# The last layer behind its mixers on 576 instead of 592 columns: the meta columns are left out

## The chip, the cores and the metric

The kernel runs on one core of a Trainium2 chip. The metric is the device time of one launch in microseconds. TensorE (PE) multiplies, VectorE (DVE) and ScalarE (ACT) do the elementwise work, GpSimd (POOL) and SyncE (SP) issue the transfers.

## The reference, cut to what matters

Two layers of a decoder trunk run over a prompt of 512 tokens with 16 learned meta tokens ahead of it, and over 8 sample sequences of 8 tokens that share the weights: 64 + 16 + 512 = 592 tokens, which are the columns of every activation in the kernel. Each layer is

```python
h = h + 0.5 * swiglu(rmsnorm(h, w['norm_ffn1']), ...)
x = rmsnorm(h, w['norm_mix']);  z = x @ w['w_in'] + w['b_in']
# four mixers: conv, retention, gated linear attention (GLA), differential attention
gate = jax.nn.sigmoid(gates.reshape(B, L, N_BRANCH, D_MODEL))
merged = jnp.einsum('blnc,ncd,blnd->bld', branches, w['w_branch'], gate)
h = h + merged @ w['w_out']
h = h + 0.5 * swiglu(rmsnorm(h, w['norm_ffn2']), ...)
...
y_prompt = h_p[:, N_META:]
```

The meta tokens are dropped from the result `y`. In the mixers they are keys, values and states that the later tokens read, and their keys and values are outputs of both layers; behind the mixers of the last layer nothing reads them.

## The kernel before

Activations lie transposed: 128 partitions hold a tile of 128 channels, and the 592 tokens are the columns, ordered sample (64, `TS`), meta (16, `META`), prompt (512). A product runs in two halves of `HALF` = 296 columns, one PSUM bank each. Every float32 product is made of three reduced products (high times high, low times high, high times low), so each value exists as a high and a low part: `x_hi`/`x_lo` (the layer's input), `w_hi`/`w_lo` (a weight unit of 8 blocks of 128x128), `hid_hi`/`hid_lo`, `br_hi`/`br_lo`, `m_hi`/`m_lo`. ScalarE makes the high part, VectorE the low one.

SP streams the weights, 512 KB a unit, into a ring of four slots (`w_raw`); `split_high` (ACT, L773) and `split_low` (DVE, L1984) prepare a unit, TensorE multiplies it in `products` (L1362): 8 blocks x 3 products x 2 halves = 48 matmuls. The feed-forwards use another scheme (`ffn`, L1391): for each of 22 pairs of gate and up tiles seven products of 4 blocks x 3 matmuls, on operands that are sums and differences of the two halves of the columns (`x_half`, tiles of `HALF` columns in `x_hi`, `x_lo` and `x_more`), with VectorE forming the sums of weights and the quarters of the result. The steady pairs run in a hardware loop.

The order of a layer, written out by hand for each engine and tied by semaphores: first feed-forward and its down projection (3 units for each of 8 output tiles), `project` (values, then 18 tiles of `z`), attention of the samples, attention of the prompt, retention, GLA, head norms, merge, output projection, second feed-forward, its down projection. Of the 32 tiles of branch gates 24 are "early": TensorE makes them block by block between the steps of the mixers (`early_gates`, L1362 through `products`), ScalarE takes their tanh into `hT[:, 0:4]` (`gate_activated`, L1117), and SP stores them to DRAM (`gate_rows`) and fetches them back for the merge; the first five tiles of the residual `hT` are spilled to `h_rows` meanwhile. In `gates` each of 8 output tiles takes a late gate tile (48 matmuls) and the products of the four branches (4 x 12), merged by VectorE (L2793, L2798, L2803). `head_norms` sums squares over heads by products with a matrix of ones (`sum_tile`, L1374, full float32, two records each), ScalarE makes the inverse roots.

At the end `last_tiles` (DVE) adds the last output tile in two halves (L2318, L2320), and SP stores `y_out` tile by tile behind the last weight load (L639), the last tile in two halves (L641, L643).

`product` in `ffn`, `products` and `sum_tile` set TensorE's widths; in the other engines each operation names its own slice (`room`, `HALF`, `T`).

## Time and profile before

| | us |
|---|---|
| median of three runs | 2823.16 |
| lowest, highest | 2822.53, 2825.8 |
| the profiled execution | 2824.82 |
| its span, first to last instruction | 2823.2 |

The profile is of one execution, so its times are summed against its own 2824.82 us. In a timeline a row's second number is the duration of the merged group, which for pipelined matmuls overlaps the next one: the time of one matmul is better taken from the length of a run divided by its count. "<-" behind an idle time names what ended it.

### The profile page before, as it was taken

The page shows a single profiled execution, that of the slowest core. Times are in us where ns is not written, and L with a number is a line of the kernel's source. Part 1 is how long each engine was busy: PE and PEld are TensorE (multiplying, and loading weights), DVE is VectorE, ACT ScalarE, POOL GpSimd, SP SyncE. Part 2 cuts the span into 40 slices and gives each one's busy share as a digit, 9 for nine tenths or more (in the row PEclk, how much of TensorE's full clock was granted, in tenths as well). Part 3 has the DMA queues.
Part 4 walks back from the last instruction along what each step waited for, and adds up shares of the span by engine and source line. Part 5 has one row for each costly group of instructions (what it writes and reads, how often), then busy time and mean ns, then how long its engine had stood idle before and what let it go on. Part 6 is the DMA issues. An engine that isn't in the chain of part 4 may idle for free.

```text
span 2823.2 us, 57804 instructions
## 1 busy us (share of the span) xinstructions
PE 2798.5 (99%) x21860; PEld 2711.6 (96%) x21860; DVE 1992.6 (71%) x3588; ACT 1208.0 (43%) x2156; POOL 120.6 (4%) x218
## 2 busy tenths in 40 slices
PE   8999999999999999999999999999999999999999
PEld 7999999988899999999999999999888899999999
DVE  8889534477667688886488894346776676988942
ACT  6445323435334254454254462234353433554521
POOL 0000001230000000000000000012300000000000
PEclk9999999999999999999999999999999999999999
DMA  4222325562234312223222232255623343122232
GB/s 137 98 95 97 105 67 190 159 225 90 98 112 168 123 54 95 98 89 112 82 72 92 89 105 97 93 166 172 214 87 113 126 153 108 68 89 89 104 99 101
DMA packets 103024, 320.00 MB, mean 113 GB/s; under 512 B 13615, under 2 KB 30415, under 8 KB 101312
## 3 DMA queue, kind: packets, MB, share of 16 engines
q1 hardware_dynamic: 90576, 277.03, 28.5%
q0 software_dynamic: 12272, 40.56, 4.5%
q8 instruction: 119, 1.95, 0.3%
q14 instruction: 57, 0.47, 0.1%
HBM read 289.76 MB, written 29.12 MB: 113 GB/s over the span
## 4 chain that ended last, share of the span: by engine, by line
PE 96%; DVE 2%; SPq 1%; issue 1%; ACT 1%; DMA 0%; DVEq 0%; ACTq 0%
PE ps L1362 50%; PE ps L1391 35%; PE ps L1568 3%; PE ps L1374 2%; PE ps L1637 1%; PE ps L1849 1%; PE ps L1670 0%; PE ps L1715 0%; PE ps L1735 0%; DVE Z L2496 0%; PE ps L1689 0%; DMA w_raw<-wstream 0%; PE ps L1619 0%; PE ps L1796 0%; SPq L563 0%
## 5 line engine op out<-in xcount | busy, mean ns | idle before, releaser
L1984 DVE TENSOR_TENSOR w_lo<-w_raw,w_hi 128x1024 fp32r<-128x1024 f32 x240 | 292.6, 1224 | 355.1 <-ACT w_hi L773 351.6
L1391 PE MATMUL ps<-x_more,w_hi 128*128 128x296 f32 x2112 | 459.3, 299 | 1.5 <-DVE x_more L2846 1.1
L1391 PE MATMUL ps<-x_hi,w_hi 128*128 128x296 f32 x1408 | 420.6, 299 | 1.3 <-DVE w_lo L2022 1.2
L1391 PE MATMUL ps<-x_hi,w_lo 128*128 128x296 f32 x1408 | 421.6, 299 | 0.0
L1391 PE MATMUL ps<-x_lo,w_hi 128*128 128x296 f32 x1408 | 421.4, 299 | 0.0
L773 ACT ACTIVATE w_hi<-w_raw 128x1024 fp32r<-128x1024 f32 x224 | 234.6, 1053 | 411.4 <-PE ps L1362 243.3
L1362 PE MATMUL ps<-x_hi,w_hi 128*128 128x296 f32 x1600 | 364.9, 309 | 2.8 <-ACT hT L1117 2.8
L2022 DVE TENSOR_TENSOR w_lo<-w_raw,w_hi 128x512 fp32r<-128x512 f32 x440 | 296.9, 689 | 91.2 <-ACT w_hi L821 91.2
L1391 PEld LDWEIGHTS ps<-x_more,w_hi 128*128 128x128 f32 x2112 | 351.0, 188 | 2.7 <-issue 1.6
L1362 PE MATMUL ps<-x_lo,w_hi 128*128 128x296 f32 x1600 | 348.8, 299 | 0.0
L1362 PE MATMUL ps<-x_hi,w_lo 128*128 128x296 f32 x1600 | 348.2, 299 | 0.0
L1391 PE MATMUL ps<-x_more,w_lo 128*128 128x296 f32 x1056 | 314.9, 298 | 0.0
L1362 PE MATMUL ps<-hid_hi,w_hi 128*128 128x296 f32 x1408 | 310.8, 300 | 0.0
L1362 PE MATMUL ps<-hid_hi,w_lo 128*128 128x296 f32 x1408 | 308.9, 298 | 0.0
L1362 PE MATMUL ps<-hid_lo,w_hi 128*128 128x296 f32 x1408 | 308.5, 298 | 0.0
L871 ACT ACTIVATE p_copy<-ps 128x296 f32<-128x296 f32 x264 | 110.1, 418 | 394.8 <-PE ps L1391 394.3
L1362 PEld LDWEIGHTS ps<-x_hi,w_hi 128*128 128x128 f32 x1600 | 258.6, 189 | 18.8 <-issue 14.0
L821 ACT ACTIVATE w_hi<-w_raw 128x512 fp32r<-128x512 f32 x440 | 265.5, 623 | 14.4 <-PE ps L1362 13.8
L1391 PEld LDWEIGHTS ps<-x_hi,w_hi 128*128 128x128 f32 x1408 | 265.7, 189 | 2.3 <-DVE w_lo L2022 1.7
L1391 PEld LDWEIGHTS ps<-x_hi,w_lo 128*128 128x128 f32 x1408 | 265.9, 189 | 0.0
L1391 PEld LDWEIGHTS ps<-x_lo,w_hi 128*128 128x128 f32 x1408 | 264.9, 188 | 0.0
L1362 PEld LDWEIGHTS ps<-x_hi,w_lo 128*128 128x128 f32 x1600 | 260.5, 189 | 0.0
(371 smaller groups left out, 4948.0 us busy)
## 6 DMA issues: line engine op xcount, KB each, us to landing
w_raw<-wstream SPq DMA_DIRECT2D x420, 512.0 KB, 3.7
kpage<-cache_k SPq DMA_DIRECT2D x128, 128.0 KB, 2.8
vpage<-cache_v POOLq DMA_DIRECT2D x128, 128.0 KB, 3.6
gate_rows<-hT SPq DMA_DIRECT2D x48, 296.0 KB, 2.9
d_sg<-gate_rows SPq DMA_DIRECT2D x16, 888.0 KB, 5.0
h_rows<-hT SPq DMA_DIRECT2D x2, 1480.0 KB, 6.3
hT<-h_rows SPq DMA_DIRECT2D x2, 1480.0 KB, 6.6
hT<-h_in SPq DMA_DIRECT2D x4, 592.0 KB, 8.5
```

Source lines behind the costliest of these rows:

```text
L773: act.activation(w_hi[:, slot, :, :], w_raw[:, slot, :, :], ACT.Copy).then_inc(weights_high, 1)
L821: act.activation(w_half(t)[0], w_source(t, g, total), ACT.Copy).then_inc(operands_high, 1)
L871: act.activation(room, ps[:, bank, 0:HALF], ACT.Copy).then_inc(pair_taken, 1)
L1362: mm = pe.matmul(ps[:, 2 * p + half, 0:HALF], wp[:, k, :], xp[:, k0 + k - blocks[0], half * HALF:(half + 1) * HALF], start=start and k == ...
L1374: mm = pe.matmul(ps[:, 2 * p + half, 0:HALF], mat, tile[:, half * HALF:(half + 1) * HALF], start=start, stop=stop)
L1391: mm = pe.matmul(ps[:, bank, 0:HALF], wp[:, k, :], xp, start=new and k == 0 and n == 0, stop=k == KH - 1 and n == 2, skip_group_check=True)
L1568: mm = pe.matmul(ps[0:n, (WINDOWS * g + w) % 8, 0:256], xp[:, k, c0:c0 + n], wp[:, s0:s0 + 2, k, :], start=k == 0 and m == 0, stop=k == KD ...
L1637: mm = pe.matmul(ps[0:n, score_bank(j, g, i), 0:min(ns, 512)], q, k[:, 0:min(ns, 512)], start=True, stop=True)
L1849: mm = pe.matmul(ps[0:cols, h, a0:a0 + count], g_kl[32 * h:32 * h + 32, n % 2, c0:c0 + cols], g_ql[32 * h:32 * h + 32, n % 2, at:at + coun ...
L1984: v.tensor_tensor(w_lo[:, slot, :, :], w_raw[:, slot, :, :], w_hi[:, slot, :, :].bitcast(F32), ALU.subtract).then_inc(weights_low, 1)
L2022: v.tensor_tensor(lo, w_source(t, g, total), hi.bitcast(F32), ALU.subtract).then_inc(weight_steps, 1)
```

## The change

With `MOVED` = 576, every engine keeps a variable `width` that is 296 and becomes 288 (`live_half(l)`) in the last layer when the engine enters the head norms; the early gates take 288 from the start. All slices behind that point use `span()` for `HALF` and `live(ap)` for a whole row of `2 * span()` columns. Since the 16 meta columns lie at 64 to 79, the last 16 prompt columns (576 to 591) are copied into their place at three points: the operands `x_hi`, `x_lo` (ScalarE, behind the last projection tile), the branch tiles in `Z` and `od` (ScalarE, before the head norms), the residual `hT` (VectorE, at the end of the merge). TensorE waits for the first two. The output keeps its layout: SP stores each tile of `y` as 576 columns and the moved 16 columns apart.

```diff
+MOVED = T - META
+def live_half(l):
+    return HALF if l + 1 < DEPTH else MOVED // 2
...
+        width = [HALF]
+        def live_columns(l):
+            width[0] = live_half(l)
+        def span():
+            return width[0]
+        def live(ap):
+            return ap[:, 0:2 * span()]
...
         def pair(p):
-            return ps[:, 2 * p:2 * p + 2, 0:HALF]
+            return ps[:, 2 * p:2 * p + 2, 0:span()]
...  sync
+            live_columns(DEPTH - 1)
             for m in range(KD - 1):
                 sp.wait_ge(residual_added, 4 + 24 * DEPTH - KD + m + 1)
-                sp.dma_start(y_out[:, m:m + 1, :], hT[:, m:m + 1, :]).then_inc(y_stored, 16)
+                sp.dma_start(y_out[:, m, 0:MOVED], hT[:, m, 0:MOVED]).then_inc(y_stored, 16)
+                sp.dma_start(y_out[:, m, MOVED:T], hT[:, m, TS:TS + META]).then_inc(y_stored, 16)
             sp.wait_ge(first_half_added, 1)
-            sp.dma_start(y_out[:, KD - 1, 0:HALF], hT[:, KD - 1, 0:HALF]).then_inc(y_stored, 16)
+            sp.dma_start(y_out[:, KD - 1, 0:span()], hT[:, KD - 1, 0:span()]).then_inc(y_stored, 16)
+            sp.dma_start(y_out[:, KD - 1, MOVED:T], hT[:, KD - 1, TS:TS + META]).then_inc(y_stored, 16)
             sp.wait_ge(residual_added, 4 + 24 * DEPTH)
-            sp.dma_start(y_out[:, KD - 1, HALF:T], hT[:, KD - 1, HALF:T]).then_inc(y_stored, 16)
-            sp.wait_ge(y_stored, 16 * (KD + 1))
+            sp.dma_start(y_out[:, KD - 1, span():MOVED], hT[:, KD - 1, span():MOVED]).then_inc(y_stored, 16)
+            sp.wait_ge(y_stored, 16 * (2 * KD + 1))
...  scalar, tile(l, c)
+                    if l == DEPTH - 1 and c == NZ - 1:
+                        act.activation(x_hi[:, :, TS:TS + META], x_hi[:, :, MOVED:T].bitcast(F32), ACT.Copy)
+                        act.activation(x_lo[:, :, TS:TS + META], x_lo[:, :, MOVED:T].bitcast(F32), ACT.Copy).then_inc(z_ready, 1)
...  scalar, head_norms(l)
                 act.wait_ge(lvl_scores, len(level_items))
+                if l == DEPTH - 1:
+                    act.wait_ge(conv_done, 1)
+                    act.wait_ge(prompt_evac, 10)
+                    act.wait_ge(ret_evac, WINDOWS)
+                    act.wait_ge(gla_evac, WINDOWS)
+                    act.activation(Z[:, RQ:CA, TS:TS + META], Z[:, RQ:CA, MOVED:T], ACT.Copy)
+                    act.activation(od[:, :, TS:TS + META], od[:, :, MOVED:T], ACT.Copy).then_inc(gla_evac, 1)
+                    act.wait_ge(gla_evac, WINDOWS + 1)
+                live_columns(l)
...  tensor
-                            mm = pe.matmul(ps[:, 2 * p + half, 0:HALF], wp[:, k, :],
-                                           xp[:, k0 + k - blocks[0], half * HALF:(half + 1) * HALF],
+                            mm = pe.matmul(ps[:, 2 * p + half, 0:cols], wp[:, k, :],
+                                           xp[:, k0 + k - blocks[0], half * cols:(half + 1) * cols],
...
-                            mm = pe.matmul(ps[:, bank, 0:HALF], wp[:, k, :], xp, start=new and k == 0 and n == 0,
+                            mm = pe.matmul(ps[:, bank, 0:span()], wp[:, k, :], xp, start=new and k == 0 and n == 0,
...
-                    last = products(gate_pair(f), slot, (part, part + 1), part, x_hi, x_lo, start=part == 0, stop=part == 7)
+                    last = products(gate_pair(f), slot, (part, part + 1), part, x_hi, x_lo, start=part == 0, stop=part == 7, n_cols=live_half(l))
...
                         pe.wait_ge(z_ready, NZ + 1)
+                        if l == DEPTH - 1:
+                            pe.wait_ge(z_ready, NZ + 2)
...
                 pe.wait_ge(conv_done, 1)
+                if l == DEPTH - 1:
+                    pe.wait_ge(gla_evac, WINDOWS + 1)
+                live_columns(l)
...  vector
             def head_norms(l):
+                live_columns(l)
...
                 v.wait_ge(h_back, 16)
+                if l == DEPTH - 1:
+                    v.tensor_copy(hT[:, :, TS:TS + META], hT[:, :, MOVED:T])
                 v.drain().then_inc(mixers_left, 1)
```

The rest of the diff replaces `HALF` by `span()`, `HALF:T` by `span():2 * span()` and whole rows by `live(...)` in the steps behind the mixers.

## Rows read from the trace of the kernel before

**Rows 1.** The page: busy us (share) xinstructions, then the clock by slice.
```profile
PE 2798.5 (99%) x21860; PEld 2711.6 (96%) x21860; DVE 1992.6 (71%) x3588; ACT 1208.0 (43%) x2156; POOL 120.6 (4%) x218
PEclk9999999999999999999999999999999999999999
```

**Rows 2.** Busy us by stretch: PE, PEld, DVE, ACT, POOL; then clock, DMA.
```profile
2424.00:2676.00 252.00, 252.00 (x1850) 251.74 (x1849) 227.15 (x405) 132.82 (x257) 0.00 (x0) 1.00 0.26 92
sum 740.00, PE 739.74 PEld 717.66 DVE 519.30 ACT 300.91 POOL 4.98; mean PE 105.68 PEld 102.52 DVE 74.19 ACT 42.99 POOL 0.71
```

**Rows 3.** The chain that ended last, its end: start us, us, what.
```profile
2259.55 164.05 PE ps L1362 x1200
2423.60 8.17 PE ps L1391 x60
2431.77 1.00 PE ps L1374 x4
2432.76 243.48 PE ps L1391 x1788
2676.24 143.75 PE ps L1362 x1056
```

**Rows 4.** The chain in the projection of layer 1: the values, 256 columns.
```profile
1828.45 37.08 PE ps L1568 x315
```

**Rows 5.** Waits of TensorE from 1992 to 2260 us: total, times, longest.
```profile
PE ps L1362 <- ACT hT L1117: 1.4, 3, 0.6
...
PE ps L1796 <- DVE rst L2587: 0.2, 1, 0.2
```

**Rows 6.** Timeline of ScalarE in the head norms, and the chain's ones-sums there.
```profile
2234.97 2.45 ACT L1221 ACTIVATE Z<-Z 128x592 f32<-128x592 f32 x4
2246.06 0.66 ACT L1229 ACTIVATE hn_root<-ps 128x592 f32<-128x592 f32 x1 [1.93 <-PE ps L1374]
...
2241.04 7.97 PE ps L1374 x32
```

**Rows 7.** Timelines of ScalarE and TensorE around the last projection tile.
```profile
2014.10 0.75 ACT L1041 ACTIVATE Z<-ps,prm 128x592 f32<-128x592 f32 x1 [4.97 <-PE ps L1362]
2016.52 0.28 ACT L1096 ACTIVATE s_turn<-ps 128x128 f32<-128x128 f32 x1 [0.15 <-PE ps L1691]
...
2016.38 0.54 PE L1362 MATMUL ps<-x_hi,w_hi 128*128 128x296 f32 x2
2017.31 0.27 PE L1701 MATMUL ps<-ident,s_turn 128*128 128x128 f32 x1
```

**Rows 8.** Timeline of VectorE where the output projection begins.
```profile
2377.71 0.78 DVE L2257 SCALAR_TENSOR_TENSOR hT<-ps,hT 128x592 f32<-128x592 f32 x1 [1.54 <-PE ps L1362]
```

**Rows 9.** Timelines of VectorE and TensorE in the first pair of feed-forward two.
```profile
2438.38 0.69 DVE L2022 TENSOR_TENSOR w_lo<-w_raw,w_hi 128x512 fp32r<-128x512 f32 x1
...
2439.19 0.32 PE L1391 MATMUL ps<-x_hi,w_hi 128*128 128x296 f32 x1
```

**Rows 10.** VectorE's tile groups behind 2260 us, and its idle time in a pair.
```profile
L2137 DVE TENSOR_TENSOR tmp<-ps,p_copy 128x296 f32<-128x296 f32 x44 | 20.2, 459 | 0.0
L2142 DVE TENSOR_TENSOR tmp<-tmp,gu 128x592 f32<-128x592 f32 x22 | 16.9, 769 | 0.0
...
2567.82 0.69 DVE L2022 TENSOR_TENSOR w_lo<-w_raw,w_hi 128x512 fp32r<-128x512 f32 x1 [0.94 <-ACT w_hi L821]
```

**Rows 11.** SP's issues at the end, its wait, and the slowest small load's landing.
```profile
2800.20 5.47 SPq L639 DMA_DIRECT2D y_out<-hT  x7
2812.09 0.33 SPq L641 DMA_DIRECT2D y_out<-hT  x1
SPq L643 <- DVE hT L2320: 8.6, 1, 8.6
aw<-params POOLq DMA_DIRECT2D x2, 8.0 KB, 8.9
```

**Rows 12.** Timeline of VectorE: a slice of 528 of 592 columns.
```profile
1985.71 0.76 DVE L2496 SCALAR_TENSOR_TENSOR Z<-Z,prm 128x528 f32<-128x528 f32 x1
```

More of the change, by code:

```diff
@@ L870, in copy @@
                 def copy(room, bank):
-                    act.activation(room, ps[:, bank, 0:HALF], ACT.Copy).then_inc(pair_taken, 1)
+                    act.activation(room[:, 0:span()], ps[:, bank, 0:span()], ACT.Copy).then_inc(pair_taken, 1)
                 def pair_(N, quad, j, kind, tile):
@@ L1116, in gate_activated @@
                 c = f // EARLY + 8 * (f % EARLY)
-                act.activation(split_cols(hT[:, f % STAGES, :]), pair(gate_pair(f)), ACT.Tanh, scale=0.5, bias=hb[:, c:c + 1]).then_inc(gate_tanh, 1)
+                n, bank = live_half(l), 2 * gate_pair(f)
+                act.activation(hT[:, f % STAGES, 0:2 * n].rearrange("p (h t) -> p h t", h=2), ps[:, bank:bank + 2, 0:n], ACT.Tanh, scale=0.5,
+                               bias=hb[:, c:c + 1]).then_inc(gate_tanh, 1)
             def gate_high(l, f):
@@ L1310, in _ @@
                     lower(k, P_GAIN)
-                x_high_of("B22", k, hT[:, KH + k, HALF:T], gain_of(P_GAIN, KH + k))
+                x_high_of("B22", k, hT[:, KH + k, span():2 * span()], gain_of(P_GAIN, KH + k))
                 if k == 1:
@@ L1354, in _, with products @@
         def _(pe):
-            def products(p, slot, blocks, k0, xh, xl, start=True, stop=True, wh=None, wl=None, halves=range(2)):
+            all_columns()
+            def products(p, slot, blocks, k0, xh, xl, start=True, stop=True, wh=None, wl=None, halves=range(2), n_cols=None):
                 wh = w_hi[:, slot, :, :] if wh is None else wh
                 wl = w_lo[:, slot, :, :] if wl is None else wl
+                cols = span() if n_cols is None else n_cols
                 for k in range(blocks[0], blocks[1]):
@@ L1373, in sum_tile @@
                 for half in range(2):
-                    mm = pe.matmul(ps[:, 2 * p + half, 0:HALF], mat, tile[:, half * HALF:(half + 1) * HALF], start=start, stop=stop)
+                    mm = pe.matmul(ps[:, 2 * p + half, 0:span()], mat, tile[:, half * span():(half + 1) * span()], start=start, stop=stop)
                 return mm
@@ L1750, in retention @@
                 for half in range(2):
-                    mm = pe.matmul(ps[:, 4 + half, 0:HALF], aw[96:112, :], GL[:, half * HALF:(half + 1) * HALF], start=True, stop=True)
+                    mm = pe.matmul(ps[:, 4 + half, 0:span()], aw[96:112, :], GL[:, half * span():(half + 1) * span()], start=True, stop=True)
                 mm.then_inc(alpha_product, 1)
@@ L2102, in second_tile @@
                 v.wait_ge(x_parts, parts(L, f, "t3", k) - 1)
-                difference(k, gain, t2, t3, t3 if f or last else side[:, :], parts(L, f, "t3", k))
+                difference(k, gain, t2, t3, t3 if f or last else side[:, 0:span()], parts(L, f, "t3", k))
                 if last:
                     lower(L, f, k, gain)
-                x_low_of(L, f, "B22", k, hT[:, KH + k, HALF:T], gain_of(gain, KH + k))
+                x_low_of(L, f, "B22", k, hT[:, KH + k, span():2 * span()], gain_of(gain, KH + k))
                 x_low_of(L, f, "T2", k, t2, None)
@@ L2165, in pair_ @@
                         sum_three(N + 1, g)
-                    quarter(N, 0, tmp[:, 0, HALF:T], BANK_E, a_copy, after)
+                    quarter(N, 0, tmp[:, 0, span():2 * span()], BANK_E, a_copy, after)
                     quarter(N, 1, c22, j, e_copy, after)
@@ L2170, in pair_ @@
                     low(N + 1, W_S1, g, w_sum)
-                    quarter(N, 2, tmp[:, 0, 0:HALF], BANK_B, first_copy[j], after)
+                    quarter(N, 2, tmp[:, 0, 0:span()], BANK_B, first_copy[j], after)
                     sum_two(N + 1, g, w_sum)
@@ L2212, in ffn @@
                 split_low(quad0 + KF // 2, 0)
-                quarter(N, 0, tmp[:, 0, HALF:T], BANK_E, a_copy)
+                quarter(N, 0, tmp[:, 0, span():2 * span()], BANK_E, a_copy)
                 quarter(N, 1, c22, 1, e_copy)
                 hidden_low(1, 3)
-                quarter(N, 2, tmp[:, 0, 0:HALF], BANK_B, first_copy[1])
+                quarter(N, 2, tmp[:, 0, 0:span()], BANK_B, first_copy[1])
                 hidden_low(3, 6)
@@ L2316, in last_tiles @@
                         v.wait_ge(last_half, 1)
-                    cols = slice(half * HALF, (half + 1) * HALF)
-                    v.tensor_tensor(tmp[:, 1, cols], ps[:, 2 * OUT_PAIRS[3] + half, 0:HALF], inverse[:, cols], ALU.mult).then_inc(out_scaled, 1)
+                    cols = slice(half * span(), (half + 1) * span())
+                    v.tensor_tensor(tmp[:, 1, cols], ps[:, 2 * OUT_PAIRS[3] + half, 0:span()], inverse[:, cols], ALU.mult).then_inc(out_scaled, 1)
                     v.wait_ge(out_scaled, l * 16 + 8 + KD + half)
@@ L2870, in _ @@
                     for n in range(3):
-                        opening_low("B21", n, hT[:, KH + n, 0:HALF], gain_of(P_GAIN, KH + n), 1 + LATE_PARTS if n == 2 else 1)
+                        opening_low("B21", n, hT[:, KH + n, 0:span()], gain_of(P_GAIN, KH + n), 1 + LATE_PARTS if n == 2 else 1)
                     low(0, W_S3, 0, w_sum_first)
```

92 lines of the change are left out of this document (49 added, 43 removed).

## The prediction

> **What bounds the kernel now.** I read the page first, then the busy time by stretch, then the chain of work that ended last, then the waits of the engines beside TensorE. In the page the reader is to see that TensorE's matmuls fill 99% of the span at a granted clock of nine tenths or more in every slice, VectorE 71%, ScalarE 43% [rows 1]. Such a share is an average, so the stretches of the last layer come next: from 2080 us to 2820 us the matmuls fill everything but 0.26 us of 740 us, at clock 1.00 (the 2.4 GHz level), while VectorE is at 227 of 252 us in the second feed-forward and far lower elsewhere [rows 2]. The chain says the same: behind the head norms it is three unbroken runs of matmuls, 1,200 + 1,848 + 1,056 of them, and then 2.8 us of VectorE and a store [rows 3]. So the price of a column is TensorE's, as long as nothing else becomes late.
>
> **What a column costs.** The trace holds no matmul of this kind with 288 columns, so its price is bounded by neighbours. 1,788 matmuls of 296 columns took 243.48 us, 136.17 ns each [rows 3]. 315 of 256 columns, also with a weight load each, took 37.08 us, 117.71 ns each [rows 4]. The line through both has 18.46 / 40 = 0.4615 ns a column, and almost no constant (296 x 0.4615 = 136.6), so 8 columns are worth 3.69 ns of each matmul. The other bound is the clock alone: 8 / 2.4 GHz = 3.33 ns, which holds if the some 12 ns above 296 / 2.4 = 123.3 ns are not proportional. The 256-column matmuls read other operands, so the line isn't proof; I still take 3.69, the rows being the nearest there are, and keep 3.33 as the low end. That a matmul at 256 columns starts every 117.7 ns also shows that the weight load beside it doesn't set the pace at 132 ns.
>
> The Trainium skill (TensorE: Matmul & The Clock Gate, Back-to-back issue gap) gives N / 2.4 GHz + 2.5 ns for a warm matmul. That would be 125.8 ns at 296 columns where the trace has 136.2, so the trace doesn't agree on the level; by the rule's slope the sum below would be 1.9 us smaller.
>
> **The change part by part.**
> 1. Late gates, branch products, output projection (384 + 384 + 384), second feed-forward (22 pairs x 7 products x 12 = 1,848), its down projection (8 x 22 x 6 = 1,056): 4,056 matmuls. All lie in runs without a gap [rows 3], so all of it is on the path: 4,056 x 3.69 = 14.97 us (low end 13.5).
> 2. The 24 early gates are 24 x 48 = 1,152 matmuls of the same kind, worth 4.25 us at most. They fill TensorE's time between the mixers' steps, and where TensorE then waits the saving is lost. Its waits there are 3.2 us in all, in four groups of which the first and the last stand in [rows 5]. The largest, 1.4 us in three waits, are round trips (last matmul of a gate, then ScalarE's tanh that empties the banks, then TensorE), which keep their length and move forward with the shorter gate. Others, as the wait for VectorE's update of the retention state, the last of the four, swallow what the gate matmuls ahead of them save. I take 4.0 us; with a quarter lost and the low price it is 2.9.
> 3. The ones-sums of the head norms and of the last RMS norm: 52 records (32 and 16 in the head norms, 4 in the last norm) of 249 ns at 296 columns [rows 3, 6], in proportion 249 x 8 / 296 = 6.7 ns each, 0.35 us.
> 4. Added on ScalarE, behind the last projection tile: two copies of 128 x (8 x 16) values of the operands. The nearest row is a 128x128 copy of 0.28 us, so 0.56 us together. Queued behind them are the split of a weight unit, two exponentials and the copy of the sample attention's output. TensorE's new wait for the copies stands before the first gate, which starts at 2016.38; the tile's own activation ends near 2014.8, so the copies are done 1 us before. The copy that starts at 2016.52, 0.15 us after its input, can slip by 0.4 us; six gate matmuls cover it until the transpose at 2017.31 [rows 7]. Exposed: 0, at worst 0.5.
> 5. Added on ScalarE before the head norms: two more copies (192 and 32 values a partition) and a wait for its own semaphore, priced by the same 0.28 us row, some 0.7 us in all. Behind them stand four tanh, four squares and a gate. TensorE asks for the copies only after eight gate blocks, at 2241.04, where ScalarE was past this point at 2235; ScalarE's later idle 1.93 us before the first root takes up the rest [rows 6]. Exposed: 0, at worst 0.5.
> 6. Added on VectorE at the end of the merge: one copy of the residual's 16 columns, 0.2 to 0.3 us by the same row, queued in front of the first residual addition. VectorE is idle 1.54 us there, waiting for the first output tile [rows 8]. Cost 0, also for the drain; the cover is gone only if the copy takes over 1.5 us.
> 7. Where a stall could appear: the opening of the second feed-forward. VectorE works without a break from the last output tile on and finishes the low part of one weight operand at 2439.07; TensorE uses it from 2439.19 [rows 9]. Over this stretch TensorE gets some 115 x 3.69 ns = 0.42 us faster, VectorE's 21 tile operations some 0.2 us, by (769 - 459) / 296 = 1.05 ns a column [rows 10]. So about 0.1 us of waiting in the first pair; at worst 0.4. In the steady pairs VectorE is idle 0.94 us of each 11.43 us [rows 10] and TensorE has no wait, so 0.31 us less a pair is covered.
> 8. Stores: SP issues 17 instead of 9. Seven were issued between 2800.20 and 2805.67; doubled, at the same price, they end near 2811.1, ahead of the first half of the last tile at 2812.09, and SP then waits 8.6 us for the last half [rows 11]. The new pieces are 64 bytes a partition. The rows have no such store; priced between nothing and the 8.9 us that the slowest small load took to land [rows 11], the last piece, issued near 2812, has landed by 2821.5, before the last half store, which lands at the span's end. Cost 0. The stores of gate rows and their loads stay full width. Of the tail, two VectorE operations lose 8 columns each, 0.02 us.
>
> The Trainium skill (DMA: Bandwidth & Descriptors, Specifications) says that pieces under 512 bytes are read, modified and written; this speaks against the 64-byte stores, and no row here prices it. It would change nothing in the sum unless a piece took over 10 us.
>
> Sum: 14.97 + 4.0 + 0.35 - 0.1 (point 7) - 0.1 (a share of points 4 and 5) = 19.1 us. The profiled execution took 2824.82 us with a span of 2823.2 us, 1.66 us more than the median of the three runs; the sum is taken off either alike: 2805.7 for the profiled execution, 2823.16 - 19.1 = 2804.1 us for the median.
>
> **The rivals.**
> - The column is worth 3.33 ns (the clock alone). For it: a matmul's extra 11 to 13 ns could belong to the operands' layout. Against: it would have to grow by 1.8 ns between 256 and 296 columns by chance. 13.5 + 3.7 + 0.35 - 0.2 = 17.3 us, 2805.8 us.
> - Waits take the gates' share: the shorter gates no longer cover VectorE's and ScalarE's steps in the mixers, and the added copies are exposed. For it: ScalarE and VectorE chains of 2 to 4 us stand behind every block of gates. Against: the blocks shrink by 0.04 to 0.18 us, and TensorE hardly waits [rows 2, 5]. 14.97 + 1.5 + 0.35 - 1.3 = 15.5 us, 2807.7 us.
> - Column counts are served in steps of 16: 296 costs as 304, 288 as 288. Then the slope is 18.46 / 48 = 0.385 ns and the step 6.15 ns: 24.9 + 6.7 + 0.4 - 0.5 = 31.5 us, 2791.7 us. Nothing excludes it, nothing points to it: the constant left over would be 19 ns.
> - Slower: VectorE becomes the bound of the feed-forward because the narrowed slices (576 of 592 columns) run at half pace. A pair has 3 quarters, 2 halves and 2 full tiles, 3.8 us of busy time; doubled, the pair would take some 14.1 us on VectorE, 22 x (14.1 - 11.4) = 59 us more, and the other stages give back 19.1 - 6.8 = 12 us: near 2870 us. It decides from a pair of 12.3 us on. Against: a slice of 528 of 592 columns takes 0.76 us, a full row 0.77 us [rows 10, 12].
> - The change doesn't do what it says: a part keeps 296 columns. All the helpers named in the diff take their width from one place, so a part left out would be small; within the low end.
>
> **How the numbers follow.** The forecast, 2804.1 us, 0.64; the clock price, 0.22; waits 0.09; steps of 16, 0.03; VectorE at half pace 0.01; effects without a name, of either sign, 0.01. The range must hold the first three with the runs' own spread (0.6 us below to 2.6 us above the median), and leaves out most of the others: 2802.5 to 2808.0. A measurement of this kernel can tell 0.2% (5.6 us) from no change; all cases but the slow one are beyond it: faster 0.97, same 0.02, slower 0.01.
>
> **What would show each step.** In the changed kernel the runs of 1,200, 1,788 and 1,056 matmuls should last near 159.6, 236.9 and 139.9 us, 132.5 ns a matmul; 132.8 would be the clock price, 130 the step. The span from the first gate (2016.4) to the end of the head norms should shrink by 4.0 + 0.3 us. TensorE's waits should stay near 3 us in the mixers, with at most 0.3 us new in the first feed-forward pair. ScalarE's four and VectorE's one new copies should be under 0.4 us each with no TensorE wait behind them. The last store should be issued 0.03 us after VectorE's last operation. Layer 0 and the projections of layer 1 should not change. A span that shrinks by less than 16 us or more than 21 would make the prediction wrong, and the first number to look at then is the time of one matmul.

## The result and the profile after

The changed kernel took 2805.57 us (median of four executions, 2802.11 to 2806.43); the kernel before, run beside it, 2823.65 us (median of four, 2822.53 to 2825.8). The two medians differ by 18.1 us. The ratio on record is 0.9923, 95% interval 0.9911 to 0.9935; it isn't the quotient of these medians (0.9936), and the record doesn't show how it is formed. On 2823.16 us it means 21.7 us less (18.4 to 25.1). The forecast was 19.1 us less, to 2804.1 us, and by the ratio the time lies at 2801.4 us (2798.0 to 2804.8), below the foot of the range. So the direction was right, but these executions alone can't tell a saving of 19 us from one of 22: they scatter more than the forecast had room for. The runs below settle the size, 20.75 us, which is more than was forecast, and show what the scatter is. All executions spoken of are of the same state; what scatters them by 1 to 10 us are short drops of the granted clock of TensorE, which are a subject of their own further down.

The profiled execution took 2806.43 us with a span of 2804.8 us (before: 2824.82 and 2823.2). First the busy time of its page, which answers to [rows 1]:

```profile
PE 2780.5 (99%) x21860; PEld 2693.5 (96%) x21860; DVE 1986.4 (71%) x3589; ACT 1206.9 (43%) x2160; POOL 119.6 (4%) x218
```

The counts show the change as written: TensorE has as many instructions as before, VectorE one more (the copy of the residual), ScalarE four more (the operand and branch copies). TensorE lost 18.0 us of busy time, the span 18.4 us. The end of the chain, start and duration in us, answers to [rows 3]:

```profile
2239.19 7.76 PE ps L1421 x32
...
2257.18 158.90 PE ps L1409 x1200
...
2425.01 236.96 PE ps L1438 x1788
2661.97 139.66 PE ps L1409 x1056
```

The reader is to compare three lengths. The run of 1,200 fell from 164.05 to 158.90 us (4.29 ns a matmul), that of 1,788 from 243.48 to 236.96 us (3.65 ns), that of 1,056 from 143.75 to 139.66 us (3.87 ns). But the run of 1,200 starts only 2.37 us earlier than before, where the early gates and the ones-sums should have brought over 4. The granted clock by stretch says why (busy us of PE, PEld, DVE, ACT, POOL, then the clock, DMA share, GB/s):

```profile
2212.00:2216.00 4.00, 4.00 (x17) 3.92 (x17) 1.11 (x4) 0.00 (x0) 0.00 (x0) 0.50 0.47 158
2216.00:2220.00 4.00, 4.00 (x25) 2.99 (x24) 0.49 (x2) 2.07 (x3) 0.00 (x0) 0.76 0.19 76
...
820.00:824.00 4.00, 4.00 (x25) 3.36 (x25) 0.00 (x0) 1.42 (x2) 0.00 (x0) 0.77 0.17 69
```

In two places, in the gated attention of layer 1 and of layer 0, TensorE was at the 1.2 GHz level for some us although the profile shows no wait of it there (4.00 of 4.00 us busy; the ends of matmuls are modelled in a trace, so gaps of some ns inside a row of them wouldn't show): with the slices beside the ones shown (0.88 from 2208, 0.80 from 816) some 7 us in the first place and 3.4 us in the second, if a slice at 0.50 was at the lower level throughout. That is the whole of what its mean clock of 0.998 leaves for the lower level; the rest ran at 2.4 GHz. The profile of the kernel before has such a drop in one place, in the retention of layer 0:

```profile
744.00:748.00 4.00, 4.00 (x29) 3.23 (x29) 1.86 (x2) 0.00 (x0) 0.00 (x0) 0.78 0.39 85
```

So comparing these two profiled executions by their spans mixes the change with one drop against two.

### The profile page after: what moved, and what is told of

Read it like the earlier page. It is cut to its first block, busy times and chain, and to the rows that moved or that the text cites. A ratio compares the mean times of both kernels' runs of the same rounds, so it can differ in the third digit from the quotient of the medians.

```text
span 2804.8 us, 57820 instructions
## 1 busy us (share of the span) xinstructions
PE 2780.5 (99%) x21860; PEld 2693.5 (96%) x21860; DVE 1986.4 (71%) x3589; ACT 1206.9 (43%) x2160; POOL 119.6 (4%) x218
## 3 DMA queue, kind: packets, MB, share of 16 engines
q8 instruction: 119, 1.95, 0.3%
## 4 chain that ended last, share of the span: by engine, by line
PE 97%; DVE 2%; ACT 0%; issue 0%; DMA 0%; SPq 0%; DVEq 0%; ACTq 0%
PE ps L1409 51%; PE ps L1438 35%; PE ps L1615 3%; PE ps L1421 2%; PE ps L1684 1%; PE ps L1898 1%; PE ps L1717 1%; PE ps L1736 0%; PE ps L1764 0%; PE ps L1784 0%; DVE Z L2550 0%; DMA w_raw<-wstream 0%; PE ps L1666 0%; PE ps L1917 0%; PE ps L1845 0%
## 5 line engine op out<-in xcount | busy, mean ns | idle before, releaser
L1438 PE MATMUL ps<-x_more,w_hi 128*128 128x296 f32 (+1 forms) x2112 | 456.8, 298 | 1.4 <-DVE x_more L2903 1.0
L1438 PE MATMUL ps<-x_hi,w_hi 128*128 128x296 f32 (+1 forms) x1408 | 419.5, 298 | 1.2 <-DVE w_lo L2076 1.2
L1438 PE MATMUL ps<-x_hi,w_lo 128*128 128x296 f32 (+1 forms) x1408 | 420.0, 298 | 0.0
L1438 PE MATMUL ps<-x_lo,w_hi 128*128 128x296 f32 (+1 forms) x1408 | 419.8, 298 | 0.0
L1409 PE MATMUL ps<-x_hi,w_hi 128*128 128x296 f32 (+1 forms) x1600 | 363.0, 308 | 2.8 <-ACT hT L1151 2.8
L1409 PE MATMUL ps<-x_hi,w_lo 128*128 128x296 f32 (+1 forms) x1600 | 347.3, 298 | 0.0
L1409 PE MATMUL ps<-x_lo,w_hi 128*128 128x296 f32 (+1 forms) x1600 | 347.2, 298 | 0.0
L1438 PE MATMUL ps<-x_more,w_lo 128*128 128x296 f32 (+1 forms) x1056 | 314.2, 298 | 0.0
L1409 PE MATMUL ps<-hid_hi,w_hi 128*128 128x296 f32 (+1 forms) x1408 | 309.1, 298 | 0.0
L1409 PE MATMUL ps<-hid_hi,w_lo 128*128 128x296 f32 (+1 forms) x1408 | 307.5, 297 | 0.0
L1409 PE MATMUL ps<-hid_lo,w_hi 128*128 128x296 f32 (+1 forms) x1408 | 307.5, 297 | 0.0
L901 ACT ACTIVATE p_copy<-ps 128x296 f32<-128x296 f32 (+1 forms) x264 | 109.7, 416 | 389.2 <-PE ps L1438 388.7
L1409 PEld LDWEIGHTS ps<-x_hi,w_hi 128*128 128x128 f32 x1600 | 258.2, 189 | 19.1 <-issue 14.1
```

Source lines behind the costliest of these rows:

```text
L901: act.activation(room[:, 0:span()], ps[:, bank, 0:span()], ACT.Copy).then_inc(pair_taken, 1)
L1409: mm = pe.matmul(ps[:, 2 * p + half, 0:cols], wp[:, k, :], xp[:, k0 + k - blocks[0], half * cols:(half + 1) * cols], start=start and k == ...
L1438: mm = pe.matmul(ps[:, bank, 0:span()], wp[:, k, :], xp, start=new and k == 0 and n == 0, stop=k == KH - 1 and n == 2, skip_group_check=True)
```

## The experiments

Two terms first. A "drop" is a stretch in which TensorE's granted clock is at the lower level; an execution is called undisturbed when its mean granted clock is 1.000, that is, when it has no drop.

**The theory** behind the runs: the price of 8 columns is not one number; it is 4.3 ns in the products that read the layer's input and under 4 ns in the others, so the change is worth some 21 us, nothing that it adds is exposed, and the scatter comes from drops of the clock that it neither causes nor cures. **The rivals**: the copies, waits and stores cost or gain something; the gain includes work that moved, not only columns; the second half of a tile starts at another place and that, not the count, makes it cheaper; the drops are part of the change.

**The changed kernel again.** No edit.

> The changed kernel, unedited, in more runs. The theory (8 columns are worth 3.7 to 4.3 ns of each of 5,208 matmuls, and each drop of the granted clock in the mixers costs 2 to 3 us, in either kernel) expects 19 to 22 us less than the kernel before in the same rounds, and that single runs of both kernels differ by steps of 2 to 3 us that go with the clock listed for them (1.000, 0.999, 0.998). The rival (the shorter gates make TensorE sparser and so cause the extra drop seen in the GLA stage) expects the changed kernel to be at 0.998 in most runs where the one before is at 0.999, and 18 us less.

Measured: median 2803.34 us of six (2801.78 to 2812.19), beside it 17 executions of the kernel before with 2828.55 us (2822.67 to 2831.03); ratio 0.9924 (0.9906 to 0.9941). Each execution also has its mean granted clock. The two at 1.000 took 2801.78 and 2801.94 us, those at 0.999 took 2803.09 and 2803.59, those at 0.996 took 2812.15 and 2812.19. The kernel before is the same: four at 1.000 (2822.67 to 2822.90 us), three at 0.999 (2824.13 to 2824.30), the others at 0.998 and 0.997 (2827.26 to 2831.03). Over all sets of executions with a clock beside them 14 of 51 of the kernel before were undisturbed, with a median of 2822.71 us, and 6 of 20 of the changed kernel, median 2801.96 us. **The change is worth 20.75 us** where no drop disturbs it, and 20.6 to 20.8 us on each of the three chips taken by itself. The profile taken here was undisturbed throughout, so it is the one to read the saving from:

```profile
2023.96 3.41 PE ps L1409 x24
...
2234.69 7.76 PE ps L1421 x32
...
2252.68 158.90 PE ps L1409 x1200
...
2420.51 236.96 PE ps L1438 x1788
2657.47 139.66 PE ps L1409 x1056
```

The kernel before, the same first place of its chain (its drop was long over by then):

```profile
2025.95 3.52 PE ps L1362 x24
```

From the first line to the ones-sums (2241.04, [rows 6]) the kernel before took 215.09 us, the changed one 210.73: 4.36 us for 1,008 early gate matmuls, 4.33 ns each. From there to the end of the span it is 582.16 against 565.61 us, 16.55 us.

**The copies and waits alone.** The width stays 296 in both layers, everything else of the change is in: copies, waits, split stores.

```diff
 def live_half(l):
-    return HALF if l + 1 < DEPTH else MOVED // 2
+    return HALF
```

> The changed kernel with full widths everywhere: the copies, the new waits and the split stores stay, no slice is narrower. Theory: they are hidden, so the time is that of the kernel before within 0.5 us (ratio 0.9998 to 1.0002). Rival (the added steps eat a part of the gain): 1 us or more above it.

Measured: 2830.1 us (11 executions, 2823.02 to 2833.03), ratio 1.0008 (0.9998 to 1.0018); its one undisturbed execution took 2823.02 us, 0.3 us above the 2822.71 of the kernel before. That is a single execution; the chain bears it out. Its run lengths are those of before to the last digit, and from the start of the run of 1,200 to the end of the span it is 563.60 us against 563.65:

```profile
2264.80 164.05 PE ps L1409 x1200
...
2438.02 243.48 PE ps L1438 x1788
2681.51 143.75 PE ps L1409 x1056
```

So what the change adds is hidden, to within 0.3 us, and the rest of the gain is width.

**The early gates wide.** Only their products and their tanh keep 296 columns.

```diff
-                n, bank = live_half(l), 2 * gate_pair(f)
+                n, bank = HALF, 2 * gate_pair(f)
...
-                    ... stop=part == 7, n_cols=live_half(l))
+                    ... stop=part == 7, n_cols=HALF)
```

> The changed kernel with the 24 early gates back at 296 columns (their products and their tanh), the rest at 288. Theory: the early gates are worth 4 to 5 us, so this takes 4 to 5 us more than the unedited changed kernel, all of it between the first gate and the end of the head norms. Rival (the waits between the mixers' steps swallow the gates' share, as the 2.4 us of the first profile suggest): 1 to 2.5 us more.

Measured: 2811.89 us (6 executions, 2807.85 to 2813.98), ratio 0.9939 (0.9925 to 0.9953); none undisturbed, so the totals bound the early gates only loosely. The chain doesn't depend on that:

```profile
2028.44 3.52 PE ps L1409 x24
...
2243.54 7.76 PE ps L1421 x32
...
2261.73 159.02 PE ps L1409 x1200
```

215.10 us from the first gate here to the ones-sums: all of the 4.36 us come back. Of the last 96 early gate matmuls, the 48 between the ones-sums give back 0.20 us (6.55 against 6.35) and the 48 that open the run of 1,200 give back 0.12 us. Counted by their share of that run's saving in the changed kernel the second 48 were worth 0.21 us, so the early gates are worth 4.36 us and another 0.32 to 0.41. The runs of 1,788 and 1,056 are those of the changed kernel.

**Narrow only from the output projection on.** `live_columns(l)` and the copies for it moved from the head norms to the output projection on all three engines; gates, branches and merge at 592 columns.

```diff
             def head_norms(l):
...
-                live_columns(l)
...
             def out_projection(l):
+                live_columns(l)
```

> Only the output projection, the second feed-forward and its down projection run on 576 columns; gates, head norms, branch products and the merge stay at 592. Theory 1 (each stage gives back its matmuls' own price of 8 columns, read from the changed kernel's profile: 4.2 ns in the products that read the layer's input, 3.65 ns in the feed-forward, 3.87 ns in the down projection): 384 x 4.2 + 1,848 x 3.65 + 1,056 x 3.87 = 12.5 us, so an execution without a drop of the granted clock takes 2822.7 - 12.5 = 2810.2 us, and the run of 1,200 matmuls splits into 816 at 136.7 ns and 384 at 132.4 ns. Theory 2 (one price of 3.69 ns for all): 3,288 x 3.69 = 12.1 us, 2810.6 us; the two are told apart by the lengths of the runs in the profile, not by the total. Theory 3 (a part of the gain is the earlier start of other work, not the price of columns): under 11 us, above 2811.7 us.

Measured: 2817.54 us (6 executions, 2812.22 to 2817.68, none undisturbed), ratio 0.9968 (0.9956 to 0.998).

```profile
2264.77 162.53 PE ps L1409 x1200
...
2436.23 236.96 PE ps L1438 x1788
2673.19 139.66 PE ps L1409 x1056
```

The run of 1,200 lost 1.52 us, all of it in the 384 matmuls of the output projection, 3.96 ns each; the other 816 (gates and branches) hold the remaining 3.63 us of the changed kernel, 4.45 ns each. From the start of that run to the end of the span it is 551.23 us against 563.65 before, 12.42 us, where theory 1 had 12.5 and theory 2 12.1. The stages give back their own columns, each at its own price; nothing in these lengths is left over for work that moved.

**The price of a width by itself.** Nine groups of 96 matmuls were put behind the last product, on the layer's input and two weight units, the results unused.

```diff
+            for cols, second, pairs in ((256, 256, 1), (288, 288, 1), (288, 296, 1), (296, 296, 1), (296, 288, 1), ...):
+                ... for each unit, k, product and half:
+                    pe.matmul(ps[:, half, 0:cols], wp[:, unit, k, :], xp[:, k, c:c + cols], start=True, stop=True)
```

> The changed kernel with nine rows of 96 matmuls each behind its last operation, of the kind of the products (a new weight load for each): columns, and start of the second half in columns: 256/256, 288/288, 288/296, 296/296, 296/288, 304/288, 320/256, then 296 and 288 with every matmul of a tile at the same start. Only the time of one matmul in each row is of interest. Theory 1 (in proportion to the columns): 117.7, 132.4, 132.4, 136.1, 136.1, 139.8, 147.2 ns. Theory 2 (clock plus a constant): 288 to 296 differ by 3.3 ns, 256 to 320 by 26.7 ns. Theory 3 (a second half that starts at 296 columns, 1,184 bytes, is off a 64-byte line and costs extra): 288/288 is faster than 288/296 and 296/288 faster than 296/296, by 0.5 ns or more.

Measured, its matmuls' starts read from the trace one by one, from the first start of a group to the first start of the next, divided by 96: 118.2 ns at 256 columns; 132.6 at 288 with the second half at 288, 132.3 with it at 296; 136.7 at 296 with the second half at 296, 136.7 with it at 288; 139.8 at 304; 146.2 at 320; and with every matmul of a tile at the same start 136.9 at 296 and 132.8 at 288. The first group is read too high: the gap behind its first matmul is 220 ns, and without it the 256 columns cost 117.2. Where the second half starts makes no difference beyond 0.3 ns where the rival asked for 0.5 or more, so that rival falls. But the step from 288 to 296 is 4.1 to 4.4 ns, and the one from 296 to 304 is 3.1 ns: not a line. A second series took every multiple of 8.

```diff
-            for cols, second, pairs in ((256, 256, 1), (288, 288, 1), (288, 296, 1), ...):
+            for cols, second, pairs in ((248, 248, 1), (256, 256, 1), (264, 264, 1), (272, 272, 1), ..., (320, 256, 1)):
```

> The changed kernel followed by ten groups of 96 matmuls (the layer's input as moving operand) of 248, 256, 264, ... 320 columns, read from the trace one by one. The first such series gave 118.2 ns at 256, 132.6 at 288, 136.7 at 296, 139.9 at 304 and 146.2 at 320. Theory 1 (a line with 0.4615 ns a column, the prediction's): 114.5, 118.2, 121.9, 125.6, 129.3, 132.9, 136.6, 140.3, 144.0, 147.7 ns. Theory 2 (the steps are unequal: columns in odd multiples of 8 cost some 0.5 to 1 ns more than the line between their neighbours): 264, 280, 296 and 312 columns stand 0.5 to 1 ns above the middle of their neighbours, the step from 288 to 296 is 4.1 ns and the one from 296 to 304 is 3.1 ns. Theory 3 (only 296 is off, by where its second half starts): the others lie on a line within 0.2 ns.

Five of its stretches, one for each group of 96, from 256 columns and then from 280 to 304 (PE busy, with the count of records that touch the stretch, then clock, DMA share, GB/s):

```profile
2809.11:2820.36 11.25, 11.25 (x99) 1.00 0.01 1
...
2844.11:2856.50 12.39, 12.39 (x99) 1.00 0.00 0
2856.50:2869.19 12.69, 12.69 (x98) 1.00 0.01 1
2869.19:2882.31 13.12, 13.12 (x98) 1.00 0.00 1
2882.31:2895.74 13.43, 13.43 (x98) 1.00 0.00 1
```

All of them, divided by 96, give 114.0 (the first gap, again 220 ns, left out; 115.1 with it), 117.1, 122.1, 125.3, 129.0, 132.2, 136.7, 139.9 and 143.7 ns from 248 to 312 columns. Steps of 8 columns cost 3.1, 5.0, 3.2, 3.7, 3.2, 4.5, 3.2 and 3.8 ns. The odd multiples of 8 (264, 280, 296, 312) cost more than the middle of their neighbours, by 0.9, 0.2, 0.6 and 0.6 ns (146.2 ns taken for 320). Theory 2 is right in kind, though 280 stays under its 0.5 ns; theories 1 and 3 are not: the slope between two measured widths 40 columns apart doesn't give the step between two widths 8 apart, and in products of this kind the change happened to leave a dear width for a cheap one. The groups all read the layer's input. The second feed-forward and its down projection, with steps of 3.65 and 3.87 ns in the kernel itself, read other operands, and no group of single widths was run on those.

**The drops of the clock.** They stand, in all profiles of the kernels so far, in the retention or the gated attention, where the decoding tokens meet their stored states: in each layer and mixer two stretches of 32 records of 8 columns. An undisturbed execution of the changed kernel (that of the run below) shows one such place:

```profile
738.42 1.10 PE L1852 MATMUL ps<-rqh,ss 64*64 64x8 f32 x32
...
740.75 1.10 PE L1852 MATMUL ps<-rqh,ss 64*64 64x8 f32 x32
```

Four edited kernels and two repeats of the changed one ask whether the narrow matmuls bring the drops (theory A) or chip and moment do (rival B), and whether a kernel without drops can be had. The first is a repeat.

> The changed kernel itself, run beside the two that move blocks, as their reference. Undisturbed executions at 2801.8 us (20.9 us under the undisturbed executions of the kernel before, 2822.7 us); others above by 1.3 to 10.4 us for one to four drops of the granted clock. If the moment decides, the share of undisturbed ones is that of the kernel before beside it.

Measured: 2806.68 us (5 executions, 2802.12 to 2810.54, one undisturbed), ratio 0.9942 (0.9929 to 0.9956); of the ten executions of the kernel before beside it six were undisturbed.

Wide matmuls in the middle of each narrow stretch:

```diff
                             for b in range(NB):
                                 ... two matmuls of 8 columns ...
+                                if b == NB // 2 - 1:
+                                    early_gates(l, 1)
```

> The changed kernel, with one block of gate matmuls (6 of 288 columns, 0.8 us) put into the middle of each stretch of 32 matmuls of 8 columns in the retention's and the gated attention's state products, in both layers; the two blocks for it are taken from the fills behind. Theory A (the granted clock falls because of the long stretches of narrow matmuls, 64 of 8 columns with one block between, behind which every drop seen so far stands): no stretch is longer than 16 products, so no window of the profile shows a clock below 1.00, and the executions gather within 1 us, at 2801.8 to 2803 us, 0 to 1 us of it a new wait for VectorE behind the thinner fills. Rival B (the drops are a matter of chip and moment, the sites are only where the check falls): drops remain, at the same sites or elsewhere, and the times spread over 2801.8 to 2812 us as before.

Measured: 2811.36 us (5 executions, 2808.86 to 2812.58), ratio 0.9954 (0.994 to 0.9967). One was undisturbed, with 2808.86 us: the rearrangement itself costs 6.9 us. Its waits (us, times, longest) show part of it: in layer 0 alone the waits for the tanh went from 1.4 to 2.4 us, and there is a new one for the gated state.

```profile
PE ps L1941 <- DVE g_st L2755: 0.6, 1, 0.6
```

And the drops stayed, at the same sites:

```profile
2220.00:2224.00 4.00, 4.00 (x21) 3.10 (x21) 0.57 (x2) 1.69 (x2) 0.00 (x0) 0.61 0.19 76
```

So breaking a stretch in two doesn't keep the drops away.

The gate block between the two stretches moved behind them:

```diff
-                            if j == 0:
-                                early_gates(l, 1)
...
                     mm.then_inc(ret_update, 1)
+                    if w == 0:
+                        early_gates(l, 1)
```

> The changed kernel with the one block of gate matmuls between the two stretches of 32 narrow matmuls moved behind them, so that 64 matmuls of 8 columns follow each other with only four small products between, in both layers. Theory A (the narrow stretches cause the drops): every execution has drops at the four sites, each 1.5 to 3.5 us, so 2806 to 2814 us with few or none at 2801.8. Rival B (chip and moment): the same spread as the changed kernel run beside it, 2801.8 to 2812 us, with the same share of undisturbed executions.

Measured: 2805.56 us (5 executions, 2804.81 to 2811.97), ratio 0.9935 (0.9921 to 0.9948). None undisturbed, and the profile has a drop in each of the four sites; but the other four, 2804.81 to 2805.95 us, are shorter than theory A's 2806 to 2814 and lie where the changed kernel's disturbed ones lie too. It settles nothing.

The narrow matmuls left out; the outputs lack the decoding tokens' read of their stored states, so some 7.3 us of the difference (2801.96 - 2794.6) is work that is missing.

```diff
-                            for b in range(NB):
-                                for r in (0, 64):
-                                    mm = pe.matmul(out[r:r + 64, NT * b:NT * b + NT], ss[r:r + 64, j, b, r:r + 64],
...
```

> The changed kernel without the matmuls of 8 columns (the decoding tokens' products with their stored states in the retention and the gated attention, both layers, 4 x 32 a layer): these contributions are left out of the outputs. The stretches of 32 took 1.10 us each, eight of them 8.8 us, of which 8 us lie on TensorE's path. Theory A (the narrow matmuls bring the drops of the granted clock): no drop in any execution, all within 0.5 us of each other, at 2801.8 - 8 = 2794 us. Rival B (the drops belong to the moment or to the whole stretch of small products around them): drops of 1.3 to 4 us stay at or near the same sites in at least half of the executions, and the times spread over 2794 to 2802 us. For the main question nothing changes: the runs of 1,200, 1,788 and 1,056 matmuls keep 158.9, 237.0 and 139.7 us.

Measured: 2794.61 us (4 executions, 2793.97 to 2794.77), all at clock 1.000; ratio 0.9886 (0.9871 to 0.9901).

```profile
744.00:748.00 4.00, 4.00 (x36) 3.37 (x36) 2.51 (x6) 0.38 (x1) 0.00 (x0) 1.00 0.72 211
...
2140.00:2144.00 4.00, 3.69 (x34) 2.91 (x33) 2.32 (x7) 1.43 (x3) 0.00 (x0) 1.00 0.21 81
```

The last row has 0.31 us in which TensorE is idle, and still the clock stays.

> The changed kernel itself again, as reference for the kernel without the narrow products: undisturbed executions at 2801.8 to 2802.1 us, others 1.3 to 10.4 us above. If theory A holds, it has drops on this chip where the kernel without narrow products has none.

Measured on the same chip as the kernel without the narrow products: 2804.84 us (5 executions, 2801.96 to 2806.47), two undisturbed, ratio 0.9923 (0.991 to 0.9937); of nine of the kernel before two undisturbed.

The narrow matmuls merged into full ones, for a faster kernel that leaves nothing out:

```diff
                             for b in range(NB):
-                                for r in (0, 64):
-                                    mm = pe.matmul(out[r:r + 64, NT * b:NT * b + NT], ss[r:r + 64, j, b, r:r + 64],
-                                                   rqh[r:r + 64, j, NT * b:NT * b + NT], ...)
+                                mm = pe.matmul(out[:, NT * b:NT * b + NT], ss[:, j, b, :],
+                                               rqh[:, j, NT * b:NT * b + NT], ...)
```

> The changed kernel with the decoding tokens' state products as 8 full matmuls a group (128 x 128 against 8 columns, the stored states being block diagonal) in place of 16 of 64 x 64 or 32 x 64: 16 records a stretch instead of 32, in both layers; nothing is left out. Theory A (the many narrow matmuls bring the drops of the granted clock): half as many, so fewer drops, most executions undisturbed. Their own price is not in the traces: 32 records of a quarter of the array took 1.10 us, 34 ns each; a 128 x 128 transpose starts every 0.11 us as two records, 55 ns each. So 16 x 34 = 0.55 us to 16 x 55 = 0.88 us a stretch, eight stretches 1.8 to 4.4 us less: an undisturbed execution near 2798.5 us (2797.4 to 2800.1). Rival B (the price and the drops hang on the time the engine spends at 8 columns, not on the number, and a full weight load costs what two quarters cost): 2801.8 us and drops as before.

Measured: 2824.2 us (11 executions, 2820.82 to 2826.78), ratio 0.9986 (0.9977 to 0.9995): all that the change had gained is gone. The stretch in the retention, and the clock in the gated attention of layer 0:

```profile
738.82 1.95 PE L1851 MATMUL ps<-rqh,ss 128*128 128x8 f32 x16
...
828.00:832.00 4.00, 4.00 (x16) 3.62 (x15) 1.11 (x4) 0.00 (x0) 0.00 (x0) 0.50 0.00 0
```

16 full records took 1.95 us at clock 1.00, 122 ns each; the expectation had 34 to 55 ns, the upper from transposes. The 32 smaller ones (64 x 64 or 32 x 64) took 1.10 us. Eight stretches make 6.8 us more, and the other 15 or so are drops: no execution was above clock 0.995, where the lowest of the 15 of the kernel before beside it was 0.996, and the profile has drops in all four sites, some 37 us at the lower level together.

Put together, by executions at clock 1.000: with the narrow stretches as they are (the kernel before, the changed one, and the three that differ from it in width alone) 21 of 94; without them 4 of 4; with them at 1.8 times their length 0 of 11. At 21 in 94, four in four would be luck once in some 400 times. That pools chips whose shares differ (4 of 17 of the kernel before on one, 6 of 10 on the next); on the chip of the kernel without them it is 4 of 14, and luck once in some 150. The 0 of 11 says little by its count, since beside it only 2 of 15 of the kernel before were undisturbed; what says more is how deep the clock fell in all eleven. So the narrow matmuls bring the drop behind them, and more time on them in one place brings a longer one. The merged kernel also changed their number and their size on the array, so that it is the time and not one of these is argued, not shown. That an execution sometimes escapes, and what decides it, stays open; it was not found by the block arrangements tried. Of these kernels only the one that leaves work out beats the changed one.

## Why the prediction was right or wrong

**Right: what bounds the kernel, and that everything added is hidden.** TensorE's columns were the price, and the undisturbed difference of 20.75 us is within 0.2 us of the sum of its runs (16.55 + 4.36, and next to nothing before). With the width left alone the change costs 0.3 us at most.

**Point 1** (14.97 us): 15.8 us, of which 1,152 x 4.29 = 4.9, 0.2 + 6.5 in the feed-forward, 4.1 in the down projection. **This step failed, and it is the term that was mis-sized**: "8 columns are worth 3.69 ns of each matmul" was drawn through two widths 40 columns apart, 256 and 296 columns [rows 3, 4], and bounded only downward, by the clock price. Over all 5,208 matmuls the runs gave 4.0 ns. In the feed-forward the term held (3.65 ns, 3.69 without the stall of point 7), in the down projection it was 3.87, in the output projection 3.96, in gates and branches 4.45. For the products that read the layer's input the groups of single widths show two reasons. 288 to 296 is a step of 4.1 to 4.5 ns where the mean over the eight steps is 3.7. And the line itself was joined from unlike matmuls, 256 columns in the projection and 296 in the feed-forward: in the groups 117.1 and 136.7 ns stand there, 3.9 ns for 8 columns. Why the feed-forward's step is smaller stays open. A high end as far above the line as 3.33 is below it, 4.05 ns, would have taken the foot of the range down by 5,208 x 0.36 = 1.9 us, to 2800.6 us.

**Point 2** (4.0 us): 4.8 us, of the same price: 4.36 + 0.41 us for 1,104 matmuls, and 0.02 us for the first 48, whose saving two waits for VectorE in the sample attention took (0.82 to 0.91 us and 0.81 to 0.90 us). The wait for the retention state, which the prediction had named, grew from 0.24 to 0.31 us and took 0.07 us of the rest. So the mechanism "where TensorE waits the saving is lost" was right; it took some 0.26 us, 0.19 of it from the first 48, and the allowance was 0.25.

**Point 3**: 0.21 + 0.11 + 0.03 = 0.35 us, as forecast.

**Points 4 and 5**: no new wait of TensorE. The operand copies took 0.30 us each, those of the branches 0.35 and 0.22, and the copy queued behind them ended at 2016.34, ahead of the transpose at 2016.70:

```profile
2014.16 0.30 ACT L1073 ACTIVATE x_hi<-x_hi 128x128 fp32r<-128x128 f32 x1
...
2016.09 0.25 ACT L1129 ACTIVATE s_turn<-ps 128x128 f32<-128x128 f32 x1
...
2016.70 0.27 PE L1750 MATMUL ps<-ident,s_turn 128*128 128x128 f32 x1
...
2233.33 0.35 ACT L1260 ACTIVATE Z<-Z 128x192 f32<-128x192 f32 x1
```

**Point 6**: the copy on VectorE took 0.22 us, and VectorE was still idle 1.12 us of the 1.54 us of [rows 8] behind it:

```profile
2370.16 0.22 DVE L2885 COPY hT<-hT 128x128 f32<-128x128 f32 x1
2371.50 0.76 DVE L2311 SCALAR_TENSOR_TENSOR hT<-ps,hT 128x576 f32<-128x576 f32 x1 [1.12 <-PE ps L1409]
```

**Point 7**: seen, at the place and the size forecast (0.1 us). VectorE finishes the low part of the weight at 2431.31, and TensorE's starts, 0.13 us apart, have one gap of 0.24. The matmul of [rows 9] at 2439.19 reads the high part; the low part's is the next, the last line here, 0.17 us behind it. So there was a stall of 0.03 us before, and it is 0.11 now:

```profile
2430.62 0.69 DVE L2076 TENSOR_TENSOR w_lo<-w_raw,w_hi 128x512 fp32r<-128x512 f32 x1
...
2431.36 0.40 PE L1438 MATMUL ps<-x_hi,w_hi 128*128 128x288 f32 x1
2431.60 0.29 PE L1438 MATMUL ps<-x_hi,w_lo 128*128 128x288 f32 x1
...
2439.36 0.30 PE L1391 MATMUL ps<-x_hi,w_lo 128*128 128x296 f32 x1
```

**Point 8**: the pieces of 64 bytes a partition landed 2.7 us after their issue, the tiles of 288 KB 3.2 us after theirs (issue, count, KB each, median us); the last store is issued at 2802.63, 0.02 us behind VectorE's last operation.

```profile
y_out<-hT SPq DMA_DIRECT2D x7, 288.0 KB, 3.2
y_out<-hT SPq DMA_DIRECT2D x8, 8.0 KB, 2.7
```

The Trainium skill (DMA: Bandwidth & Descriptors, Specifications) says that pieces under 512 bytes are read, modified and written. Here they landed in 2.7 us, sooner than the whole tiles, so whatever that costs decides nothing in this kernel.

**The rivals.** The clock price (3.33 ns) is refuted by every run of the chain (3.65 to 4.45 ns a matmul) and by the step from 288 to 296 columns (4.1 to 4.5 ns); waits took 0.26 us of the gates' share, not 2.5; VectorE at half pace is refuted by its 0.76 us for a row of 576 columns. "Steps of 16", given 0.03, was wrong in its form (8 columns never cost nothing or 6.15 ns; the steps measured are 3.1 to 5.0) but pointed at something real: odd multiples of 8 are dearer than the middle of their neighbours.

**What the prediction had no term for**: the drops of the clock. It read the clock as 1.00 from 2080 us on [rows 2] and as nine tenths in the page [rows 1], and took the spread of three executions (3.3 us) as the spread of the kernel. It is 10 us in either kernel, so a median of four carries 1 to 4 us of drops: 3.6 us in the changed kernel's here and 0.9 in the other's. That these two medians differ by 18.1 us, close to the 19.1 forecast, is therefore luck. The drops don't come from the change: 14 of 51 executions of the kernel before and 6 of 20 of the changed one were without them.

## What to carry to other kernels

Price a change of width at the two widths themselves, or at neighbours on both sides of each, and bound the price upward too; a slope over 40 columns was off by 8% for a step of 8 over all matmuls, and by a sixth in gates and branches. Before comparing two medians, sort the executions by their granted clock and compare the undisturbed ones: here that gave 20.75 us where the medians moved by 3 to 6 us from one set to the next. And when a stage is moved or rewritten, look at how long TensorE spends on very narrow matmuls in one place: it can be busy without a gap and lose its clock.

## What was new about the hardware

- The cost of a matmul by width, float32 rounded to the reduced format, a weight load with each, operand and bank changing: 114.0, 117.1, 122.1, 125.3, 129.0, 132.2, 136.7, 139.9, 143.7 ns from 248 to 312 columns in steps of 8.
- At full busy time by the profile (4.00 of 4.00 us) the granted clock fell to 0.50, the 1.2 GHz level, behind stretches of 8-column matmuls. In the four executions without them it never did, though TensorE was idle for 0.31 us of 4 there. The Trainium skill (TensorE: Matmul & The Clock Gate, HAM oscillation) tells of the clock falling where the engine waits for data; the traces here show a fall where the profile has no wait, so the busy share of the page didn't tell the clock.
- A record of a full 128 x 128 float32 matmul of 8 columns took 122 ns (a matmul here leaves two records), one of 64 x 64 or 32 x 64 took 34 ns: merging them in pairs cost 0.85 us a stretch at clock 1.00.
- The same 8 columns were worth 4.45 ns in gates and branches, 3.96 in the output projection, 3.87 in the down projection and 3.65 in the feed-forward. At 288 columns all of them stand at 132.3 to 132.5 ns; at 296 the first stand at 136.7 and the last two near 136.15. What makes that half nanosecond wasn't found.
